# A Fourier step on half the tokens: folding t with 512-t before the transform and unfolding when gating

## What is computed

```
def fourier_mix(u):
    B, N, _ = u.shape
    ug = u.astype(jnp.float32).reshape(B, N, D_GROUPS, D_GROUP_W)   # 512 tokens, 8 groups of 64
    y = jnp.fft.fft2(ug, axes=(1, 3), norm='ortho').real
    return y.reshape(B, N, BRANCH_W).astype(u.dtype)

# in odd_mixer
qn, kn, vn, gn, ud, gd = jnp.split(px, 6, axis=-1)
o_n = neighbourhood_attention(heads(qn), heads(kn), heads(vn), kc, vc, rpb)
out_x = jnp.concatenate([o_n * jax.nn.silu(gn), fourier_mix(ud) * jax.nn.silu(gd)], axis=-1)
```

## Time and profile before

| | us |
|---|---|
| median of 3 runs (lowest, highest) | 2531.35 (2530.65, 2531.72) |
| the profiled execution, its own time | 2530.41 |
| its span in the trace | 2528.7 |
| PE busy (matmuls) | 2335.9, 92% of the span |
| DVE busy | 1411.4, 56% |
| ACT busy | 589.1, 23% |
| POOL busy | 88.3, 3% |

### The profile page before, as it was taken

One profiled execution on the slowest core, in us unless ns is written; L12 is line 12 of the kernel. 1 busy time (PEld: TensorE's weight loads), 2 busy tenths in 40 slices (PEclk: granted clock), 3 DMA queues, 4 the chain that ended last, 5 costly groups with the idle time before them and its releaser, 6 DMA issues.

```text
span 2528.7 us, 28943 instructions
## 1 busy us (share of the span) xinstructions
PE 2335.9 (92%) x12276; PEld 1911.6 (76%) x12276; DVE 1411.4 (56%) x1673; ACT 589.1 (23%) x1138; POOL 88.3 (3%) x57
## 2 busy tenths in 40 slices
PE   6999898999899978886799999999999999999997
PEld 5787786678879744675478888889988787888886
DVE  2332346774561177565857776354388735777633
ACT  2111015661320256125621111011110001111100
POOL 0000000000000122022100000000000000000000
PEclk9899998669799989997899999999999999999998
DMA  8022130001122101120012222322222122222222
GB/s 337 18 100 100 67 117 34 18 1 51 34 84 67 68 24 57 62 72 1 34 67 85 99 100 79 103 85 84 101 82 83 65 91 97 84 100 100 79 92 79
DMA packets 30704, 196.03 MB, mean 78 GB/s; under 512 B 3440, under 2 KB 3696, under 8 KB 12528
## 3 DMA queue, kind: packets, MB, share of 16 engines
q1 hardware_dynamic: 29136, 188.03, 21.1%
q10 hardware_dynamic: 1440, 6.16, 0.7%
HBM read 192.08 MB, written 2.10 MB: 77 GB/s over the span
## 4 chain that ended last, share of the span: by engine, by line
PE 84%; DVE 11%; ACT 2%; issue 1%; POOL 1%; DMA 1%; SPq 0%; DVEq 0%; ACTq 0%; POOLq 0%
PE ps L329 20%; PE ps L330 20%; PE ps L331 20%; PE ps L385 3%; PE ps L386 3%; PE ps L387 3%; PE ps L482 2%; PE ps L556 2%; PE ps L438 2%; PE ps L767 1%; PE ps L744 1%; PE ps L587 1%; PE ps L422 1%; PE ps L920 1%; PE ps L463 1%
## 5 line engine op out<-in xcount | busy, mean ns | idle before, releaser
L1414 DVE CAST whi<-raw 128x2048 fp32r<-128x2048 f32 (+2 forms) x162 | 183.8, 1135 | 482.2 <-DMA raw<-in_ffn_out 117.4
L329 PE MATMUL ps<-h2hi,whi 128*128 128x512 f32 x1040 | 409.4, 394 | 18.3 <-DVE h2lo L1511 12.1
L330 PE MATMUL ps<-h2lo,whi 128*128 128x512 f32 x1040 | 407.0, 391 | 0.0
L331 PE MATMUL ps<-h2hi,wlo 128*128 128x512 f32 x1040 | 406.7, 391 | 0.0
L1415 DVE TENSOR_TENSOR wlo<-raw,whi 128x2048 fp32r<-128x2048 f32 (+2 forms) x162 | 341.5, 2108 | 5.6
L329 PE MATMUL ps<-h1hi,whi 128*128 128x512 f32 (+1 forms) x768 | 278.0, 362 | 16.1 <-DVE h1lo L1456 8.0
L330 PE MATMUL ps<-h1lo,whi 128*128 128x512 f32 (+1 forms) x768 | 272.7, 355 | 0.0
L331 PE MATMUL ps<-h1hi,wlo 128*128 128x512 f32 (+1 forms) x768 | 270.6, 352 | 0.0
L329 PEld LDWEIGHTS ps<-h2hi,whi 128*128 128x128 f32 x1040 | 196.7, 189 | 61.2 <-issue 13.8
L331 PEld LDWEIGHTS ps<-h2hi,wlo 128*128 128x128 f32 x1040 | 196.7, 189 | 40.9
L330 PEld LDWEIGHTS ps<-h2lo,whi 128*128 128x128 f32 x1040 | 196.9, 189 | 40.5
(11 more groups left out here) (247 smaller groups left out, 3583.4 us busy)
## 6 DMA issues: line engine op xcount, KB each, us to landing
raw<-in_ffn_in SPq DMA_DIRECT2D x44, 1024.0 KB, 4.8
raw<-in_ffn_out SPq DMA_DIRECT2D x32, 704.0 KB, 4.1
raw<-in_even SPq DMA_DIRECT2D x16, 1024.0 KB, 6.9
mod_w<-in_mod SPq DMA_DIRECT2D x6, 2048.0 KB, 25.6
mraw<-in_mod SPq DMA_DIRECT2D x12, 1024.0 KB, 4.9
raw<-in_odd SPq DMA_DIRECT2D x12, 1024.0 KB, 4.9
raw<-in_sgu_v SPq DMA_DIRECT2D x12, 1024.0 KB, 4.8
raw<-in_sgu_u SPq DMA_DIRECT2D x12, 1024.0 KB, 4.8
```

Of the source, the lines that this page charges most:

```text
L329: pe.matmul(o, r(lhi), r(rhi), start=first, stop=False, **kw)
L330: pe.matmul(o, r(lhi), r(rlo), start=False, stop=False, **kw)
L331: return pe.matmul(o, r(llo), r(rhi), start=False, stop=last, **kw)
L1414: step(dve.tensor_copy(whi[:, slot, 0:width].bitcast(F32R), raw[:, slot, 0:width]))
```

## The change

Before the transform, tokens t and 512-t are added (for the cosine part) and subtracted (for the sine part) on DVE, so that the first stage transforms 256 sums and 256 differences (token 0 stands by itself, token 256 is treated apart). The second stage takes 256 folded tokens and gives outputs 0 to 256 of the cosine part and 1 to 255 of the sine part; the other outputs are cosine minus sine of the mirrored index, and are made when gating. In detail:

- DVE, between the splits of panels 8 and 9: two instructions of 128x4x255 that make `fold` from `oud` and its reverse, and two small copies. `fold` lies where `oot` is later written.
- PE, between panels 10 and 11: the first stage, 16 matmuls of 128 columns into banks 2 to 5. After panel 11, four matmuls of 128 columns with one weight column (token 256) into one row of bank 2. Then the second stage, for each f five matmuls: two of 255 columns (sine), two of 257 (cosine), and one of 257 with a contraction of one row (token 256), into banks 3, 4, 6 and 7. PE waits for the gates not before the scores of unit 0, but before those of unit 1.
- ACT: the constants (0.66 MB in place of 2 MB) are loaded during panel 4, before the copy of panel 4, behind a new wait for `ctx_pre1_done`; four copies of 512 columns between `odd_out(10)` and `odd_out(11)` in place of eight after the latter; one copy of one row (`fourx`); and for each f a copy of 255 columns of the sine part out of PSUM in reverse order (`mirror`). These four stand ahead of the preparation of heads 0 and 1.
- DVE when gating, for each f: cosine plus sine (255 columns), mirrored cosine minus sine (255), a copy of two columns, and the multiplication by the gate (512), in place of the one multiplication.

```diff
--- before.py
+++ after.py
@@ -170,8 +170,13 @@
         ov = place("ov", A0 + 5120, [6, 512])
         ogn, ogd, oud, oot = (place(k, A0 + 8192 + i * 2048, [4, TX]) for i, k in enumerate(("ogn", "ogd", "oud", "oot")))
         o1hi, o1lo = parts("o1hi", 0, [KT, TX]), parts("o1lo", 4096, [KT, TX])
-        dft = place("dft", 0, [2, 4, TX])
-        four = place("four", 4096, [4, 1024])
+        dft = place("dft", 12288, [1285])
+        dft_cos, dft_sin = (dft[:, i * 514:i * 514 + 514].rearrange("p (t n) -> p t n", t=2) for i in range(2))
+        dft_mid = dft[0:1, 1028:1285]
+        fourx = place("fourx", 13600, [512])
+        four = place("four", A0 + 16384, [2, 1024])
+        fold = oot
+        mirror = [temp[:, TA + i * 512:TA + i * 512 + 512] for i in range(3)]
         bias_t = [place(f"bias_t{i}", 10240 + i * 960, [15, 64]) for i in range(2)]
 
         h2hi, h2lo = parts("h2hi", 0, [KT, TX]), parts("h2lo", 4096, [KT, TX])
@@ -237,7 +242,7 @@
                                            "copied", "pv", "out", "zeroed", "hi", "lo", "bias_in", "bias", "mixed",
                                            "biased")}
         o_free = sem("odd_free")
-        fo = {k: sem(f"fourier_{k}") for k in ("const", "half", "copied", "full", "out")}
+        fo = {k: sem(f"fourier_{k}") for k in ("const", "folded", "half", "copied", "full", "out")}
         y_free = {k: sem(f"{k}_free") for k in ("out0", "out1", "wo", "ffn0_out", "sgu_out", "ffn1_out")}
         v_free, kdup = sem("v_copied"), sem("k_doubled")
         alibi_ready, dist_in = sem("alibi_ready"), sem("dist_in")
@@ -253,6 +258,8 @@
         EVEN_MOVES = [2 if t < 4 else 1 for _, t, _ in EVEN_UNITS]
         moved = [sum(EVEN_MOVES[:u]) for u in range(len(EVEN_UNITS) + 1)]
         ROPE = [(side, j) for j in range(4) for side in range(2)]
+
+        FOUR_BANK = (3, 4, 6, 7)
 
         block = ctx.enter_context(nc.Block())
 
@@ -723,28 +730,38 @@
             pe.wait_ge(o_free, 8)
             token_panel(p0 + 9, 3, 6, h1hi, h1lo)
             feature_panel(p0 + 10, (6, 7), None, h1hi, h1lo)
-            pe.wait_ge(o_free, 9)
+            pe.wait_ge(fo["folded"], 4)
+            pe.wait_ge(o_free, 10)
+            for t in range(2):
+                for f in range(4):
+                    for c in range(2):
+                        at = f % 2 * 256 + c * P
+                        last = pe.matmul(ps[:, 2 + 2 * t + f // 2, at:at + P],
+                                         fold[:, f, c * 256 + t * P:c * 256 + t * P + P],
+                                         small[:, c * P:c * P + P], start=True, stop=True)
+                    if f % 2:
+                        last.then_inc(fo["half"], 1)
             feature_panel(p0 + 11, (0, 1), None, h1hi, h1lo)
-
+            pe.wait_ge(fo["copied"], 1)
+            for f in range(4):
+                last = pe.matmul(ps[0:1, 2, f * P:f * P + P], oud[:, f, 256:257], small[:, 0:P], start=True, stop=True)
+            last.then_inc(fo["half"], 1)
+            pe.wait_ge(fo["const"], 16)
+            pe.wait_ge(fo["copied"], 4)
+            pe.wait_ge(o_free, 11)
+            for f in range(4):
+                b = FOUR_BANK[f]
+                for t in range(2):
+                    pe.matmul(ps[:, b, 257:512], four[:, t, f * 256 + P:f * 256 + 2 * P], dft_sin[:, t, 0:255],
+                              start=t == 0, stop=t == 1)
+                for t in range(2):
+                    pe.matmul(ps[:, b, 0:257], four[:, t, f * 256:f * 256 + P], dft_cos[:, t, :],
+                              start=t == 0, stop=False)
+                if f == 0:
+                    pe.wait_ge(fo["copied"], 5)
+                pe.matmul(ps[:, b, 0:257], fourx[0:1, f * P:f * P + P], dft_mid, start=False, stop=True)\
+                    .then_inc(fo["full"], 1)
             pe.wait_ge(o_free, 12)
-            n = 0
-            for t in range(4):
-                for f in range(4):
-                    if n >= 8:
-                        pe.wait_ge(fo["copied"], n // 2 - 3)
-                    last = pe.matmul(ps[:, n // 2 % 4, n % 2 * 256:n % 2 * 256 + 256], oud[:, f, t * P:(t + 1) * P],
-                                     small[:, :], start=True, stop=True)
-                    last.then_inc(fo["half"], 1)
-                    n += 1
-            pe.wait_ge(fo["const"], 16)
-            pe.wait_ge(fo["copied"], 8)
-            for f in range(4):
-                for t in range(4):
-                    for c in range(2):
-                        last = pe.matmul(ps[:, 4 + f, :], four[:, t, f * 256 + c * P:f * 256 + c * P + P],
-                                         dft[:, c, t, :], start=t == 0 and c == 0, stop=t == 3 and c == 1)
-                last.then_inc(fo["full"], 1)
-            pe.wait_ge(fo["out"], 4)
 
 
             def odd_scores(u):
@@ -770,6 +787,7 @@
                     last.then_inc(oa["pv"], 1)
 
             odd_scores(0)
+            pe.wait_ge(fo["out"], 4)
             odd_scores(1)
             odd_scores(2)
             for u in range(32):
@@ -1189,11 +1207,18 @@
             for kt in range(KT):
                 act.wait_ge(c_full, kt + 1)
                 copy(h1hi[:, kt, TX:TA], sq[kt % 2][:, TX:TA], bias=modc[1][:, kt, 1:2]).then_inc(c_hi, 1)
-            for k in range(4, 12):
+            act.wait_ge(c_ok["pre1"], KT)
+            act.dma_start(dft[:], dram["dft512"]).then_inc(fo["const"], 16)
+            for k in range(4, 11):
                 odd_out(k)
+            for b in range(4):
+                act.wait_ge(fo["half"], b + 1)
+                copy(four[:, b // 2, b % 2 * 512:b % 2 * 512 + 512], ps[:, 2 + b, :]).then_inc(fo["copied"], 1)
+            odd_out(11)
+            act.wait_ge(fo["half"], 5)
+            tell(copy(fourx[0:1, :], ps[0:1, 2, :]), fo["copied"], 5)
             p0 = FIRST["odd"]
             act.wait_ge(panel_done, p0 + 12)
-            act.dma_start(dft[:], dram["dft512"]).then_inc(fo["const"], 16)
 
             def load_bias(h):
                 if h:
@@ -1203,9 +1228,11 @@
                 act.dma_start(bias_t[h % 2][:], dram["rpb"][h, :, :, :]).then_inc(oa["bias_in"], 16)
 
             load_bias(0)
-            for b in range(8):
-                act.wait_ge(fo["half"], 2 * b + 2)
-                tell(copy(four[:, b // 2, b % 2 * 512:b % 2 * 512 + 512], ps[:, b % 4, :]), fo["copied"], b + 1)
+            for f in range(4):
+                act.wait_ge(fo["full"], f + 1)
+                if f == 3:
+                    act.wait_ge(fo["out"], 1)
+                copy(mirror[f % 3][:, 257:512], ps[:, FOUR_BANK[f], 511:256:-1]).then_inc(fo["copied"], 1)
             act.dma_start(small[:], dram["dist"]).then_inc(dist_in, 16)
             def odd_hi(h):
                 a, s, t = h % 2 * 64, h % 2, h // 2
@@ -1707,7 +1734,15 @@
             split_at(p0 + 4)
             ctx_inverse(1)
             ctx_pre_norm(h1hi, h1lo, lambda kt: amul[:, kt, 1:2], lambda kt: modc[1][:, kt, 1:2])
-            for k in range(5, 12):
+            for k in range(5, 9):
+                split_at(p0 + k)
+            dve.wait_ge(o_free, 6)
+            mirrored = oud[:, :, 511:256:-1]
+            dve.tensor_tensor(fold[:, :, 1:256], oud[:, :, 1:256], mirrored, ALU.add).then_inc(fo["folded"], 1)
+            dve.tensor_tensor(fold[:, :, 257:512], oud[:, :, 1:256], mirrored, ALU.subtract).then_inc(fo["folded"], 1)
+            for i in range(2):
+                dve.tensor_copy(fold[:, :, 256 * i:256 * i + 1], oud[:, :, 0:1]).then_inc(fo["folded"], 1)
+            for k in range(9, 12):
                 split_at(p0 + k)
             dve.wait_ge(panel_done, FIRST["odd"] + 12)
             step(dve.memset(sq[0], 0.0))
@@ -1716,9 +1751,16 @@
                 dve.tensor_copy(wlo[other:other + 64, OSTK[s], TA:2 * TA].bitcast(F32R), sq[0][other:other + 64, :])\
                     .then_inc(oa["zeroed"], 1)
 
+            dve.wait_ge(o_free, 12)
             for f in range(4):
+                b = FOUR_BANK[f]
                 dve.wait_ge(fo["full"], f + 1)
-                tell(dve.tensor_tensor(ogd[:, f, :], ogd[:, f, :], ps[:, 4 + f, :], ALU.mult), fo["out"], f + 1)
+                dve.wait_ge(fo["copied"], f + 6)
+                cosines, both = ps[:, b, 0:257], mirror[f % 3]
+                step(dve.tensor_tensor(both[:, 1:256], cosines[:, 1:256], both[:, 511:256:-1], ALU.add))
+                step(dve.tensor_tensor(both[:, 257:512], cosines[:, 255:0:-1], both[:, 257:512], ALU.subtract))
+                step(dve.tensor_copy(both[:, 0:257:256], cosines[:, 0:257:256]))
+                tell(dve.tensor_tensor(ogd[:, f, :], ogd[:, f, :], both, ALU.mult), fo["out"], f + 1)
 
 
             def odd_max(u):
@@ -2002,8 +2044,12 @@
     n = np.arange(TX)
     b = 2 * np.pi * (np.outer(n, n) % TX) / TX
     scale = 1 / math.sqrt(TX * 64)
-    dft512 = np.stack([np.cos(b) * scale, np.sin(b) * scale]).astype(f)
-    dft512 = dft512.reshape(2, 4, P, TX).transpose(2, 0, 1, 3)
```

(6 more changed lines are left out.)

## The result

| | us |
|---|---|
| the change: median of 4 runs (lowest, highest) | 2514.24 (2510.98, 2514.94) |
| before, beside it on the same chip: median of 4 (lowest, highest) | 2531.0 (2529.27, 2531.72) |
| ratio, with its 95% interval | 0.9934 (0.9921 to 0.9947) |
| the profiled execution of the change, its own time | 2514.94 |
| its span in the trace | 2513.2 |

Faster by 16.8 us in the medians; 2513.7 had been forecast. One execution of the same kernel in experiment 1 took 3312.98 us at a mean granted clock of 0.641, where the others had 0.932, and its ratio there leaves it out.

The account below looks back on a forecast made before the run. PE's wait chain was taken as the bound, with 37.74 us before the first scores. New terms of 19.4 plus 0.7 for the clock make 20.1: gain 17.6, so 2512.8 profiled, 2513.7 median; 8-in-10 range 2510.7 to 2518.5.

Parts of the forecast that it names:

- What bounds, and what is saved: Panel 11's end to first scores: 37.74 us of serial work bounds; a 17.6 us gain there is kept to the end.
- The second stage: PE's matmuls after token 256: 40 records by 0.22 us, plus 0.06 for the last one's end, 8.9 us.
- Rival 1: Fourier step: mirrored and odd-placed accesses are slow; second stage 8.4 us longer, or gates as late, 2522 us; chance 0.07.
- The serial chain behind the second stage: Second stage to first scores: ACT's last mirrored copy 0.4, head 0's rows 2.2, POOL's low parts 3.1 us, plus hand-overs.
- The bias: Head 0's bias, before the first scores: requested at 861.1, ready with mask at 866.9; pessimistically 872.1, 0.4 us late.
- Rival 2: Attention's start: POOL and ACT late through bias or head 1's preparation; 3 to 5 us given back, 2518; chance 0.07.
- Fold and gates free: DVE: some 2.8 us of fold fits in a 13.35 us wait for weights; gates stay hidden behind PE and POOL.
- the gates stand next in line: Before the attention: fourth gate done about 871.4, 3.6 us behind POOL's path; only unit 1 waits for it.
- The clock at the first scores: After PE's gap of some 6 us the first scores run at 1.2 GHz, costing 0.7 us more.
- Rival 3: Attention: its own waits keep the clock low, 45 to 50 us at 0.50, so slower, 2539 us; chance 0.03.
- Everything moves together: After the attention: next-stage weights are asked for by PE's progress, so later work moves earlier along with it.
- rival 4: Behind the attention: a late transfer or another clock phase gives the gain back, 2528 to 2531 us; chance 0.02.

Follow-up runs that it names:

- experiment 1: The changed kernel again, unedited; median 2515.57 us of five, ratio 0.9941 to the kernel before.
- experiments 9: The kernel before, run again unchanged as a control for its trace; median 2531.45 us of ten, ratio 0.9999.
- experiment 10: The changed kernel with two idle 128-column matmuls (0.45 us of PE) added in the first feed-forward layer; median 2512.73 us, ratio 0.9931 to the kernel before.
- Experiment 3: The changed kernel with the first stage moved back behind panel 11; median 2515.03 us, ratio 0.9938 to the kernel before.
- experiment 4: The changed kernel with second-stage matmuls varied by tile in width, odd or even start and rows of the fifth matmul (output not the reference's); one execution, 2515.79 us.
- experiment 5: The changed kernel with token 256's matmul contracting over 128 rows, 127 of them zeros, in place of one; median 2515.14 us, ratio 0.9938 to the kernel before.
- experiment 2: The changed kernel with ACT copying head 0's rows ahead of the four mirror copies; median 2511.64 us of seven, ratio 0.9931 to the kernel before.
- experiment 8: The changed kernel with DVE making the first fold seven times; one execution, 2509.34 us.
- experiments 7: The changed kernel with PE's wait for the fourth gate put back before unit 0's scores; one execution, 2513.93 us.
- experiments 6: The changed kernel with head 0's rows copied first, 128 rows for token 256 and head 0's bias requested earlier; median 2509.53 us, ratio 0.9918 to the kernel before.

## Why the prediction was right, and where it was not

- **What bounds, and what is saved.** Right. The distance between panel 11's end and the first scores, reckoned with the first stage, fell from 37.74 to 20.84 us, and the attention behind it kept its length. The two like pairs of traces (experiments 9 and 10) give 17.0 and 17.1 us for the whole change, where 17.6 were forecast. Experiment 3 shows that it is the work that counts and not its place.
- **The second stage: the term that was mis-sized.** "40 records by 0.22 = 8.8, and 0.06" measured 10.28. The error is 1.4 us, in the step that took one price for all 40 records. The 255 and 257 columns cost what 256 do (experiment 4). The eight records of one row cost 0.31 each in place of 0.22, and each neighbouring group 0.1 more, 0.38 a tile; 128 rows bring 8.94 (experiment 5). I had thought of few rows and columns as at worst no gain.
- **Rival 1, mirrored and odd-placed accesses**, is false throughout: 255 columns backwards take 0.38 on ACT and 0.42 on DVE, and an odd start in a bank the same 0.86 for four records as an even one. The Trainium skill (PSUM — Partial Sum Buffer, "Specifications (TRN2)") says that non-contiguous patterns slow matmuls significantly. An odd start doesn't count as such here; no matmul of the Fourier step has a reversed or strided pattern, so for those no run shows it either way.
- **The serial chain behind the second stage** (0.4 + 2.2 + 3.1 and hand-overs) held to 0.1 us, and experiment 2 confirms it by taking it away. The bias was ready 2.76 + 863.21 = 865.97 (866.9 forecast). Rival 2 did not come.
- **Fold and gates free.** Right: experiments 8 and 7. That the gates stand next in line, 3.6 us behind, was right to the tenth, and experiments 2 and 6 run into them.
- **The clock at the first scores**, 0.7 forecast, 0.65 measured, and later regained: the attention is 0.25 shorter all the same (where it is regained was not followed up). The low stretch lasts until 889, 14 us of the attention, but the last 10 of them were low before as well. The comparison prices only the first 3.8 us, and beyond the 0.65 they cost nothing there: from DVE's first addition to the next scores it is 4.12 us (876.99 to 881.11) and was 4.11 (894.39 to 898.50) before. What PE lost there came out of its wait for ACT, 3.51 us before and 2.92 now. The Trainium skill's price for a low stretch (TensorE: Matmul & The Clock Gate, "HAM oscillation"), low time by one minus the ratio of the clocks, would be 1.9 us for these 3.8, an estimate. Where PE is always busy the price is about right: 3.5 us at 0.51 in the attention of experiment 1 cost 1.6, where it would be 1.7 (experiment 5). Rival 3 had that price right, but the 45 us of such a stretch did not come.
- **"Everything moves together"** (rival 4, 0.02). Nearly: the medians differ by 16.8, but in the trace 2.8 of 18.3 us are given back by the phase of the clock, to which the prediction had allowed 1.5 us. Experiments 9 and 10 show that this needs nothing of the change: the kernel before can have it, the changed one with half a microsecond of padding can be without it.

The account for the profiled execution: 17.6 forecast, less 1.4 for the second stage, plus 0.7 and 0.25 for an attention that didn't grow, plus 1.15 from the entry, less 2.8 for the clock, gives 15.5, as measured. The median came within 0.6 us of the forecast, closer than its parts deserve: part of the closeness is luck, errors that cancel. Why one execution reaches the Fourier step up to 6 us sooner than another stays open; in experiment 8 most of it was there at 152 us, and I didn't trace it further.

## What to carry to other kernels

When half of a transform is folded away on an idle engine, look first at what the longer form had been covering: here 6 of 23 possible microseconds went to a preparation that used to lie beside the second stage, and moving three instructions of ACT ahead brought 3.9 us of it back in the median. Don't save rows in a float32 matmul among full ones; with zeros in their place the second stage was 1.35 us shorter, though the whole time did not show it. And before a few microseconds far from the edit are put down to it, take the trace of the unchanged kernel a second time, and shift the changed one by a fraction of a microsecond.
